# A two-layer hybrid trunk on one core: the attention steps are regrouped in pairs of units, with new homes for scores and heads

## The reference, cut to what matters

```python
s = einsum('bhiqd,bhikd->bhiqk', qb, k) * HEAD_DIM ** -0.5    # i: two score streams of 64 columns
p = softmax(s, axis=-1)
p_diff = p[:, :, 0] - lam * p[:, :, 1]
o = einsum('bhqk,bhkd->bhqd', p_diff, v)                      # 128 columns a head
o = rmsnorm(o, g_subln) * (1.0 - lam_init)
```

## Time and profile before

| | |
|---|---|
| median of 3 runs | 2636.8 us |
| profiled execution, its own time | 2638.57 us |
| its span, first to last instruction | 2636.7 us |
| PE busy | 2554.9 us, 97% |
| PE weight loads busy | 2363.0 us, 90% |
| DVE busy | 2069.8 us, 79% |
| ACT busy | 1012.5 us, 38% |
| POOL busy | 163.7 us, 6% |
| mean granted clock of TensorE | 0.994 |
| attention steps of layer 0 | 778.07 to 870.10 us |
| attention steps of layer 1 | 2155.34 to 2224.35 us |

### The profile page before, as it was taken

How to read it: one execution, slowest core, us unless ns; L and a number is a source line. 1 busy time by engine, 2 the same in 40 slices (tenths; PEclk the granted TensorE clock), 3 DMA queues, 4 the chain that set the end, 5 groups by cost and what they waited for, 6 DMA issues and landing times. The chain is left out here.

```text
span 2636.7 us, 42699 instructions
## 1 busy us (share of the span) xinstructions
PE 2554.9 (97%) x15356; PEld 2363.0 (90%) x15356; DVE 2069.8 (79%) x3414; ACT 1012.5 (38%) x1854; POOL 163.7 (6%) x314
## 2 busy tenths in 40 slices
PE   6999999999997999999999899999998998999999
PEld 5899999988965889999999799999997866989998
DVE  5688888887958388888888888777768956688885
ACT  4333433333147333422332433234324256344443
POOL 2000000020003200000000200000002003100001
PEclk8999999999999999999999999999999999999999
DMA  8234323332111113333334123343232201223332
GB/s 295 64 120 136 116 92 114 124 104 64 55 57 49 33 56 105 117 93 115 123 103 136 48 90 119 98 130 119 91 104 72 88 24 47 79 83 109 99 101 79
DMA packets 192361, 253.97 MB, mean 96 GB/s; under 512 B 7278, under 2 KB 130268, under 8 KB 192220
## 3 DMA queue, kind: packets, MB, share of 16 engines
q1 hardware_dynamic: 192220, 252.07, 30.4%
HBM read 249.95 MB, written 2.10 MB: 96 GB/s over the span
## 5 line engine op out<-in xcount | busy, mean ns | idle before, releaser
L1211 PE MATMUL ps<-h_hi,w_hi 128*128 128x384 f32 (+2 forms) x2368 | 790.5, 334 | 21.9 <-DVE h_lo L2326 18.2
L1213 PE MATMUL ps<-h_hi,w_lo 128*128 128x384 f32 (+2 forms) x2368 | 785.3, 332 | 0.0
L1212 PE MATMUL ps<-h_lo,w_hi 128*128 128x384 f32 (+2 forms) x2256 | 749.3, 332 | 0.0
L1211 PEld LDWEIGHTS ps<-h_hi,w_hi 128*128 128x128 f32 x2368 | 449.3, 190 | 53.6 <-issue 22.5
L1213 PEld LDWEIGHTS ps<-h_hi,w_lo 128*128 128x128 f32 x2368 | 449.3, 190 | 20.7
L1212 PEld LDWEIGHTS ps<-h_lo,w_hi 128*128 128x128 f32 x2256 | 428.0, 190 | 19.2 <-issue 1.0
L1811 ACT ACTIVATE w_hi<-raw 128x512 fp32r<-128x512 f32 x464 | 279.7, 626 | 420.8 <-PE ps L1213 327.8
L2468 DVE TENSOR_TENSOR w_lo<-raw,w_hi 128x512 fp32r<-128x512 f32 x464 | 307.5, 684 | 14.8 <-ACT w_hi L1811 14.8
L1211 PE MATMUL ps<-t_hi_all,w_hi 128*128 128x384 f32 x864 | 292.1, 338 | 0.0
L1213 PE MATMUL ps<-t_hi_all,w_lo 128*128 128x384 f32 x864 | 292.0, 338 | 0.0
L1212 PE MATMUL ps<-t_lo_all,w_hi 128*128 128x384 f32 x864 | 291.9, 338 | 0.0
(11 more groups left out here) (276 smaller groups left out, 3994.1 us busy)
## 6 DMA issues: line engine op xcount, KB each, us to landing
side_raw<-in_w_ada SPq DMA_DIRECT2D x240, 256.0 KB, 2.7
raw<-in_w_ffn_gate SPq DMA_DIRECT2D x44, 1024.0 KB, 5.4
raw<-in_w_ffn_up SPq DMA_DIRECT2D x44, 1024.0 KB, 5.4
raw<-in_w_ffn_down SPq DMA_DIRECT2D x44, 1024.0 KB, 5.0
raw<-in_w_in SPq DMA_DIRECT2D x14, 1024.0 KB, 5.3
ada_buf<-in_w_ada SPq DMA_DIRECT2D x12, 1024.0 KB, 12.4
raw<-in_w_out SPq DMA_DIRECT2D x8, 1024.0 KB, 5.7
raw<-in_w_in SPq DMA_DIRECT2D x8, 512.0 KB, 7.2
```

What stands on the lines that cost most here:

```text
L1211: mm(out, wh, xh, start=start, stop=False, skip_group_check=reopened)
L1212: mm(out, wh, xl, start=False, stop=False, skip_group_check=reopened)
L1213: return mm(out, wl, xh, start=False, stop=stop, skip_group_check=reopened)
```

## The change

- S of a unit goes to one of two **sets** of three banks (0 to 2, 3 to 5), in which the 2 x 768 scores lie without a gap: 512 keys of stream 0, then 256 of stream 0 and 256 of stream 1 in the middle bank, then 512 of stream 1. PE waits, ahead of the last of the four products, for its own second one (`early_keys`), as both write the middle bank. The maxima of both streams are one reduction. Units 0 and 1 both use set 0, then the sets alternate.
- PE's order is by two steps (`attention_order`). At an even step i: S(i), OT, all of O(i-3), first half of T(i-2). At an odd step: S(i), second half of T(i-3), first half of O(i-3), first half of T(i-2), second half of O(i-3), second half of T(i-2).
- ACT now copies O's result (`take_o`), and squares four units in one instruction; DVE sums the four (`sum_heads`).
- ACT copies turned heads unrounded to `a_raw`, which frees bank 6; POOL writes `h_hi` from it (`pairs_high`) and DVE `a_lo` (`head_low`), from SBUF. The output projection waits for a count of these (`heads_ready`).
- Split of "out" tile 2 is behind the steps on ACT and DVE; tiles 0 and 1 stay at i = 4, 7 and i = 5, 8.
- The results of `fourier` cycle through banks 3 to 7. So the last pointwise result (`pw`) of layer 1 lands in bank 3 (before: 6), and S2, which now needs banks 3 to 5, waits for it.

```diff
-def score_slots(l):
-    ...
+def score_sets(l):
+
+    out, last = [], {}
+    for i in range(len(units_of(l))):
+        mine = 0 if i < EARLY_UNITS else (i + 1) % 2
+        out.append((mine, 2 * last[mine] + 2 if mine in last else 0))
+        last[mine] = i
+    return out
...
+def attention_order(l, i):
+
+    u, us = i - T_LAG, units_of(l)
+    if i % 2 == 0:
+        want = [("O", u - 1, 0), ("O", u - 1, 1), ("T", u, 0)]
+    else:
+        want = [("T", u - 1, 1), ("O", u - 1, 0), ("T", u, 0), ("O", u - 1, 1), ("T", u, 1)]
+    return [x for x in want if 0 <= x[1] < len(us) and (x[2] == 0 or us[x[1]][1] == 0)]
...
-        banks = itertools.cycle(range(4, 8))
+        banks = itertools.cycle(range(3, 8))
...
+            def pairs_high(l, a_, b_):
+
+                for u in range(2 * a_, 2 * b_, 2):
+                    h, s, t = units_of(l)[u]
+                    o = mix_segs(l)[s][0] + 128 * t
+                    wait_freed(pool, ("OT", l, u))
+                    nc.gpsimd.tensor_copy(h_hi[:, h, o:o + 256], a_raw[:, h, o:o + 256]).then_inc(head_hi_done, 1)
...
                 if q % 3 == 2:
                     conv_scales(q // 3)
-                    for b in range(len(units_of(q // 3)) // BATCH):
+                    head_scales(q // 3, 0)
+                    pairs_high(q // 3, 0, 1)
+                    for b in range(1, len(units_of(q // 3)) // BATCH):
                         head_scales(q // 3, b)
+                        pairs_high(q // 3, 2 * b - 1, 2 * b + 1)
+                    pairs_high(q // 3, 2 * b + 1, 2 * b + 2)
...
-                                wait_freed(pe, ("OT", l, last_unit(l, k, s) - 1))
+                                pe.wait_ge(heads_ready, (units_before(l) + last_unit(l, k, s)) // 2 + 1)
...
-                    parts = [(st, 2 * mine[st] + half, 384 * half, 384) for half in range(2) for st in range(2)]
+                    parts = [(0, 0, 0, 0, 512), (1, 1, 256, 0, 256), (1, 2, 0, 256, 512), (0, 1, 0, 512, 256)]
...
+                    if s == 0 and (st, b) == (0, 1):
+
+                        pe.wait_ge(early_keys, latents_before(l, i) + 1)
...
                 for i in attention_steps(l):
+                    if i < len(us):
+                        score(l, i)
                     if pair_turned(l, i) is not None:
                         turn_o(l, pair_turned(l, i))
...
+                    for what, u, half in attention_order(l, i):
+                        if what == "T":
+                            turn_p(u, half)
+                        else:
+                            heads(u, half)
...
                 for i in range(EARLY_UNITS, len(us) + OT_LAG):
...
+                    if i % 2 == 0:
+                        take_o(i - O_LAG - 1)
+                        late_p(i - T_LAG - 1, 1)
+                        if EARLY_UNITS <= i - 1 < len(us):
+                            exponent(i - 1, 1)
+                        if pair_turned(l, i) is not None:
+                            head_raw(pair_turned(l, i))
+                        if i < len(us):
+                            exponent(i, 0)
+                        take_o(i - O_LAG)
+                        if 0 <= i - O_LAG < len(us) and (i - O_LAG) % BATCH == BATCH - 1:
+                            square_heads(i - O_LAG)
+                        late_p(i - T_LAG, 0)
+                        if i < len(us):
+                            exponent(i, 1)
+                    else:
+                        late_p(i - T_LAG - 1, 1)
+                        late_p(i - T_LAG, 0)
+                        if i < len(us):
+                            exponent(i, 0)
+                    if i in (4, 7):
+                        split(("out", l, (4, 7).index(i)))
+                split(("out", l, 2))
...
                     if s == 0:
-                        for st in range(2):
-                            dve_.reduce_max(nb[:, p, st:st + 1], ps[:, 2 * mine[st]:2 * mine[st] + 2, 0:384], AX.XY,
-                                            negate=True).then_inc(max_done, 1)
+                        both = pflat[:, 512 * bank:512 * bank + 2 * TOK].rearrange("p (s n) -> p s n", s=2)
...
+                def sum_heads(u):
+
+                    at_ = (u - BATCH + 1) % 8
+                    dve.wait_ge(heads_squared, (u_before + u) // BATCH + 1)
+                    dve_.reduce_sum(osq[:, at_:at_ + BATCH], ojunk[:], AX.X).then_inc(osq_done, 1)
...
-                    stt(out=a_lo[:, h, o:o + 256], in0=pt(("OT", l, u), 256), scalar=gsub[:, l:l + 1],
-                        in1=h_hi[:, h, o:o + 256].bitcast(F), op0=ALU.mult, op1=ALU.subtract)\
-                        .then_inc(bank_free[bank_of(("OT", l, u))], 1)
+                    tt(a_lo[:, h, o:o + 256], a_raw[:, h, o:o + 256], h_hi[:, h, o:o + 256].bitcast(F), ALU.subtract)\
+                        .then_inc(heads_ready, 1)
```

More of the change, by code:

```diff
@@ L466, in mix @@
         for i in attention_steps(l):
+            if i < len(u):
+                self.score(l, i)
             if pair_turned(l, i) is not None:
                 self.slot(("OT", l, pair_turned(l, i)), 6)
[L469 to L476, removed]
+            for what in attention_order(l, i):
+                if what[0] == "T":
+                    self.slot(("T", l, *what[1:]), 6)
+                elif what[2] == heads_end(l, what[1]):
+                    self.slot(("O", l, what[1]), 7)
         for i in late_units(l):
@@ L1621, in point_wise @@
                             last.then_inc(products, 1)
-                for b in range(4):
+                for b in range(3):
                     pe.wait_ge(bank_free[b], plan.before_scores[l][b])
@@ L1696, in attention, with turn_p @@
                 u_before = units_before(l)
-                for b in (4, 5):
+                for b in (3, 4, 5):
                     pe.wait_ge(bank_free[b], plan.before_att[l][b])
+                def turn_p(u, half):
+                    key = ("T", l, u, half)
+                    wait_bank(pe, key)
+                    if half == 0:
+                        pe.wait_ge(p_ready, u_before + u + 1)
+                    for n, k in enumerate(range(3 * half, 3 * half + 3) if us[u][1] == 0 else range(2)):
+                        last = nc.tensor.transpose(ps[:, 6, 128 * n:128 * n + 128], e0[u % 3][:, 128 * k:128 * k + 128], ident[:])
+                    last.then_inc(products, 1)
@@ new lines, in heads @@
+                def heads(u, half):
+                    h, s, t = us[u]
+                    wait_freed(pe, ("T", l, u, half))
+                    if half == 0:
+                        wait_bank(pe, ("O", l, u))
+                    for k in range(3 * half, 3 * half + 3) if s == 0 else range(4, 6):
+                        last = mm(ps[:, 7, 0:128], pT[:, u % 2, k if s == 0 else k - 4, :],
+                                  vN[:, k, 128 * h:128 * h + 128], start=(k == (0 if s == 0 else 4)), stop=(k == 5), skip_group_check=True)
+                    if half == heads_end(l, u):
+                        last.then_inc(products, 1)
@@ L3004, in mix @@
                         combine(i - 1)
-                    if 0 <= i - O_LAG < len(us):
-                        take_o(i - O_LAG)
-                    if i in (5, 8, 11):
-                        split(("out", l, (5, 8, 11).index(i)))
+                    if 0 <= i - O_LAG < len(us) and (i - O_LAG) % BATCH == BATCH - 1:
+                        sum_heads(i - O_LAG)
+                    if pair_turned(l, i - 1) is not None:
+                        head_low(pair_turned(l, i - 1))
+                    if i in (5, 8):
+                        split(("out", l, (5, 8).index(i)))
+                split(("out", l, 2))
                 def add_out(j, s):
```

120 lines of the change are left out of this document (43 added, 77 removed).

## The result

The changed kernel takes 2641.96 us (median of 22 runs, 2640.04 to 2647.10) against 2637.14 for the kernel before (22 runs beside them, 2634.61 to 2640.25): ratio 1.0017, 95% interval 1.0011 to 1.0024. It is slower by 4.8 us, between 2.9 and 6.3. The forecast was 2.2 us faster; the time lies just within the range given (2625 to 2642), and on the other side of zero.

The account below looks back on a forecast made before the run. PE was taken as the bound, its waits in the two attention stages being all there was to win (29.0 us). Layer 0 -3.8, layer 1 nothing, "out" +1.6: -2.2 from the median 2636.8, so 2634.6 us, range 2625 to 2642.

Parts of the forecast that it names:

- I take 1.50 unchanged: Score products S on PE: time from S to its successor stays 1.50 us, as the halves of the rows run side by side.
- The bound given: Score products S on PE: at worst the last 256-column product runs alone, 0.45 us more per S.
- S gets longer: Slower rival, 28 latent S: 0.3 us more each in the middle, +8.4, so 2643, if S takes 1.7 or more; chance 0.14.
- Layer 1's stage: Layer 1's attention steps: 67.4 us by pairs plus 1.6 for a late S2, 69.0 against 69.0, so no gain.
- The late S2: Start of layer 1's stage: S2 waits for DVE to free bank 3 of the last pointwise result, 1.6 us lost.
- Layer 0's stage: Layer 0's attention steps: 88.2 us by pairs against 92.0, so -3.8 us.
- the walk: Both attention stages: pairs of steps followed through handovers between engines at row prices; 7.5 to 7.8 us per latent pair, 8.3 with square.
- ACT's prices: ACT's queue in the steps: copy of O 0.20 us, square 0.45; first exponential 3.40 after S starts.
- The heads in "out": Last turned heads in "out": extra POOL copy at 0.6 us; about 2.8 to the next product in layer 1; together +1.6.
- The split behind the steps: Weight split of "out" tile 2: hidden behind products of tiles 0 and 1, cost nothing; up to 1.9 us a layer otherwise.
- The weave did not close: Faster rival, both stages: PE's residual waits vanish, 12 us; time 2622 if all goes, 2628 for half; chance 0.28.
- POOL did not hold DVE: Slower rival: POOL's 20 copies hold up DVE's combine; half of them on the path is +7 us, time 2641; chance 0.06.

Follow-up runs that it names:

- the kernel with the new order of the products: Changed kernel with only S's product order altered, the awaited 256-column product now first in the queue: 2638.72 us (ratio 1.0000).
- the kernel "both": Changed kernel with the awaited product of S first in the queue and units 2, 4, ... in banks 0 to 2: 2634.35 us (0.9988).
- the new sets: Changed kernel with units 2, 4, ... taking banks 0 to 2, the wait for banks 3 to 5 moving to S(3): 2639.30 us (1.0008).
- new heads alone: Kernel before with only the turned heads changed: ACT copies them unrounded, POOL rounds, DVE subtracts from SBUF a step later: 2637.47 us (1.0002).

## Why the prediction was wrong, step by step

**The step that failed: "I take 1.50 unchanged".** The text had seen the wait and asked for its own partner: "the wait of the last one is for a product of 256 columns that began first in its half". In its half of the rows it was first; in the queue it was second, behind 512 columns, and the queue's order decides. The bound given (0.45 for 256 columns alone) was nearly met: 0.33. The rival "S gets longer", chance 0.14, was the right mechanism and place, with 0.3 for each S; its condition, S to its successor at least 1.7, held at 1.82. It counted the whole excess of 28 S, 8.4 us; the runs show about 5 for 32 (3 to 6 by the medians), because about half of the S in the stages are hidden behind ACT's copy, while the early S of units 0 and 1 (4 of them, 1.3 us), which were left out, are not. With S at its old length the forecast comes out: at the same clock the kernel with the new order of the products is 2.5 us faster than the kernel before, and the forecast was 2.2. That 2641.96 lies within the range at all is luck: the range was made for other terms, and its end is 2642.

The Trainium skill ("TensorE: Matmul & The Clock Gate", section The mechanism) says that products packed into different tiles of the array keep the program's order in their ends as in their starts, a strict first in, first out; that pointed at this cost. The trace agrees as to the flag, which comes 0.03 behind the first product's end at both places of the wait; the rows' modelled ends do not, as the second product's lies 0.42 ahead of the first one's. The rule of the Trainium skill that the prediction did cite ("TensorEngine Tiling (Array Packing)", section Restrictions and Gotchas), that two row tiles may not use a bank at once, asks for the wait and says nothing of its place.

**Layer 1's stage.** Walked 67.4; with the short S it measured 68.12, pair by pair 7.70, 9.67, 8.53, 8.52, 8.75, 7.86 and a tail of 17.09 against 7.5, 9.6, 8.3, 8.7, 8.5, 7.8 and 16.9. Right, 0.7 in all. The late S2, 1.6: right, 1.67:

```profile
2157.46 0.75 DVE L2962 SCALAR_TENSOR_TENSOR h_lo<-ps,vcol,h_hi 128x512 fp32r<-128x512 f32 x1 [0.97 <-ACT h_hi L2220]
...
2158.27 1.13 PE L1719 MATMUL ps<-kT,qT 64*128 64x512 f32 x5 [1.57 <-DVE h_lo L2962]
```

**Layer 0's stage.** Walked 88.2; 90.52 as changed, 88.94 with the short S, and that with a clock fall in it. Of the gain of 3.8 at least 3.1 was there, and the long S took half of it. Pair by pair the kernel "both", the one with 88.94, has 7.7, 7.4, 6.4, 11.1, 6.9, 5.8, 9.6, 6.4, 6.4, 9.1 and a tail of 12.1; all but the fourth and fifth (18.0 together, walked 17.8, with the fall in them) are within 0.3 of the walk. The reason given for the long ones holds where it was looked for: with the new sets, the reduction for S(14), the third latent unit behind context ones, starts 2.69 behind its S in place of 1.94, so 0.75 late. The pair that the walk had at 9.3, behind ACT's split at i = 7, takes 9.8 in the changed kernel and holds the longest wait, 2.42 for the copy of O:

```profile
804.57 0.68 PE L1749 MATMUL ps<-vN,pT 128*128 128x128 f32 x4 [2.42 <-ACT onorm L2160]
```

**ACT's prices.** The copy of O was taken as 0.20 of queue and is 0.15 to 0.16 (the next row starts so much later); the square 0.45 and is 0.54; one reduction starts 1.94 behind S with the long S in place of 1.61, and is 1.76 long. The first exponential starts 3.73 behind S: the 3.40 of the text, and the 0.33. S of a context unit was taken as 0.70, which is the length of its row; from start to start it is 0.65.

```profile
2208.01 0.90 ACT L2153 ACTIVATE e<-ps,nb 128x768 f32<-128x768 f32 x1 [0.95 <-DVE nb L2974]
2208.81 0.19 ACT L2153 ACTIVATION_READ_ACCUMULATOR e<-ps,nb 128x1 f32 x1
2208.90 0.27 ACT L2160 ACTIVATE onorm<-ps 128x128 f32<-128x128 f32 x1
2209.06 0.49 ACT L2136 ACTIVATE pT<-ps 128x384 f32<-128x384 f32 x1
```

**The heads in "out": +1.6.** Measured +1.1: from turning to the next product 2.38 in layer 1 (before 1.86) and 2.05 in layer 0 (before 1.46 by the same two starts). POOL's copy was mis-sized, 0.40 and not 0.6.

```profile
2239.81 0.39 PE L1239 MATMUL ps<-h_hi,w_lo 128*128 128x512 f32 x1
2240.04 0.60 PE L1551 MATMUL ps<-ident,onorm 128*128 128x128 f32 x4
2242.42 0.50 PE L1237 MATMUL ps<-h_hi,w_hi 128*128 128x512 f32 x1 [1.78 <-DVE a_lo L3050]
...
2207.97 0.40 POOL L1205 CAST h_hi<-a_raw 128x256 fp32r<-128x256 f32 x1
```

**The split behind the steps, at nothing.** As a cost in "out" that held: PE waits 0.2 there for a weight tile, before and after. As a saving it was in the walk, not priced by itself; it is 1.5 to 1.8 a layer by the trace.

**The sum again, from the traces:** layer 0 -1.5, layer 1 +1.3 (70.34 less 69.01) and S2 +1.7, the early S +1.3, "out" +1.1: +3.9 us without clock falls, where 4.8 (2.9 to 6.3) is measured, and 2.8 to 3.3 at the same clock. The term that turned the sign is S; with the short one the same rows give -3.1 (with a fall in it), -0.9, +1.7 and +1.1, together -1.2 or, without the fall, up to -2.9. By the medians no run here tells that from nothing (the kernel with the new order of the products has 1.0000, 0.9991 to 1.0009); at the same clock that kernel has -2.5.

**The other rivals.** The weave did not close: PE still waits some 14 us in layer 0's stage with the short S. POOL did not hold DVE: the median of `combine`'s long instruction over the 32 latent units is 1.02 before and after.

What stays open: why the clock is lower in all the other kernels than in the kernel before. In the profiled execution of each, the attention stages of the two kernels in the old order (before, new heads alone) have no fall, and of the ten others eight have one or more; but over all runs the new heads alone are as low as the weave. The lower clock goes with 1.5 to 2 of the 4.8 us; what causes it no run isolates.

## What to carry to other kernels

When a product must wait for another of its own queue, place the awaited one ahead of any longer one, not merely ahead in its part of the array: here that swapped two products, took S from 1.82 to 1.49 us, and the wait itself then cost nothing. A walk through a ring of handovers can be right to 1% a stage (67.4 against 68.1 here) and the forecast still have the wrong sign, if the one price that no row shows is taken at its favourable end; where 28 or 32 copies of it stand in the sum, look first for what orders it. And long work inside such a ring (a weight split of 1.9 us on ACT) costs nearly its full length in PE's waits (1.5 to 1.8 here); outside, the products of the tile before cover it, one split fully and of two all but 1.4. Last, where two kernels differ by a few us in 2640, compare runs at the same granted clock: here the medians gave 3.2 for a change that is 5.5.

## What the runs showed of the hardware

The flag of a 64-row product whose record ends 0.42 us earlier than that of the product ahead of it came 0.03 behind the latter's end, and the load that waited for it started 0.07 behind it. With that product first in the queue the flag came 0.014 behind its own end. A wait on PE's own flag then costs nothing beside other products (S 1.49 with and without).

The clock can fall to 1.2 GHz inside an attention stage, here for about 3.4 us each time, in two kernels once for 6.8. Busy time by stretch, layer 0, in the version with both edits, and then in the one in which the split of tile 1 is moved too:

```profile
797.00:800.00 3.00, 0.25 (x3) 0.10 (x1) 2.89 (x3) 3.00 (x5) 2.39 (x8) 1.00 0.00 0
800.00:803.50 3.50, 3.50 (x14) 2.67 (x15) 2.72 (x4) 2.99 (x8) 0.84 (x3) 0.52 0.02 5
```

```profile
797.00:800.00 3.00, 2.23 (x14) 1.52 (x13) 2.93 (x5) 2.12 (x7) 2.07 (x8) 1.00 0.00 0
800.00:803.50 3.50, 2.50 (x15) 1.85 (x15) 3.43 (x6) 2.44 (x8) 2.88 (x8) 1.00 0.02 5
```

In the first, PE was busy for 0.25 of 3.00 us (it waited 2.75 for the copy of O), and the clock granted over the next 3.5 us was 0.52. In the second, PE waited 0.95 at that place, was busy for 2.23 of the 3.00 us, and the clock stayed. It is no rule: the changed kernel and the one with the new sets have a wait of 2.42 there and no fall, the one with the new order of the products has the same 2.75 (until 801.15) and no fall before 810.4, and the changed kernel's fall at 2141 came behind 6.00 busy us of 6.00.
